# Both transposes of an expert unit put side by side, and the first two projection tiles run in lockstep

## The chip, the cores and the metric

The kernel runs on one core of a Trainium2 chip (trn2). The metric is the device time of one launch in microseconds.

## The reference

One step of a hybrid decoder layer for 1,024 prompt tokens and 8 sample tokens, width 1,024, all in float32. Conditioning rows come from a small product (`silu(c) @ w_ada + b_ada`, 9 rows, 6 vectors of 1,024 each: shift, scale and gate for each of two sub-layers). Two parts of it matter here.

```python
def modulate(x, shift, scale):
    return layer_norm(x) * (1.0 + scale) + shift

proj = u @ w_in                      # u: 1032 x 1024, w_in: 1024 x 4624
...
def expert_block(args):              # rows of one block, weights of one of 32 experts
    xb, e = args
    hb = jax.nn.silu(xb @ w_gate[e]) * (xb @ w_up[e])
    return hb @ w_down[e]
```

After normalising and modulating, the tokens are projected; an RG-LRU, a state space part and an output projection follow. Then each token goes to two of 32 experts (gate and up 1,024 x 512, down 512 x 1,024), and the two results are added with their weights.

## The kernel before, in words

**The start.** The tokens are normalised and transposed to `uT` (8 slices of 128 features). The conditioning for shift and scale is computed in four pairs: `ada_pair(c)` on TensorE (L889) multiplies, VectorE adds the bias row `badaP` to give `modP` (L1176), TensorE transposes it (L902), VectorE copies it to `ssT` (L1178) and modulates slices 2c and 2c+1 (L1184). All this is `u_pair(c)` (L1174). The projection runs in a split form: each float32 operand is split in a high and a low part, and three products are made (`PARTS`). ScalarE makes the high parts (L721 of a slice, L713 `w_high` of a tile's weights) and VectorE the low ones (`u_low` L1190, `w_low` L1152). A projection tile is 128 columns of `w_in`: 8 slices of 9 matmuls (L939). Tile 0 is made slice by slice as slices come (`by_slice`), with pairs 2 and 3 of the conditioning between its slices; then tiles 1 to 7 follow, each with two pieces of late conditioning behind it (`ada`, L877: gates and the second sub-layer's rows, added to the bias `bada4` in `mod_out`, L1244), then tiles 8 to 11. Tile t uses PSUM banks and weight buffers of parity t % 2. `lam_rates` (L1121) computes small vectors that the RG-LRU needs later. SyncE issues the weight loads in the order of L410 to L433: the tile's weights for t + 2 wait for the low part of tile t, and the two late loads behind them wait for the late pair before. POOL issues the bias rows (L512 to L519) and small rows first of all.

**The expert loop.** Rows of tokens are grouped in units of 32 rows of one expert; an expert has one or more units, 82 in all here. For each unit POOL gathers the rows (L1851, a quarter of a row on each partition, started by `icur`, which VectorE copies in `gather_rows`, L2589), TensorE transposes them (`x_turn`, L2207), VectorE copies them to `xT` (`x_out`, L2577), TensorE makes gate and up in four column tiles of 32 (`gate_up`, L2219), ScalarE copies them to `hb` (L1990), TensorE transposes that (`h_turn`, L2228), ScalarE takes a tanh (L1995), VectorE makes the product in two instructions (`h_out`, L2581, L2585), TensorE multiplies with the down weights (`down`, L2237), ScalarE copies the result (L2000) and POOL scatters it (L1859). The working copy of the weights `wcur` is filled from a ring where a unit begins a new expert: ScalarE copies gate weights (L2020) and VectorE up weights (L2619, `up_copy`), each chunk when the unit before has used its old one, and VectorE the down weights (L2632, `down_copy`) when `down` of the unit before is done. VectorE also reads the plan of the next unit into registers (`up_look`). SyncE loads three gate and up slots and two down slots of the ring, waiting for these copies. The order on each engine is written out by hand; TensorE's is

```python
                        h_turn(j * 2 + b)
                        gate_up(j * 2 + (b + 1))
                        x_turn(j * 2 + (b + 2), j + 1, b)
                        down(j * 2 + b)
```

and VectorE's is `h_out`, `up_copy` (with `x_out` of the unit after next between its second and third chunk), `gather_rows`, `scatter_rows`, `down_copy`, `up_look`.

## Time and profile before

| what | value |
|---|---|
| median of 3 runs | 1520.05 us (1520.03 to 1522.19) |
| the profiled execution | 1519.19 us, its span 1517.4 us |
| TensorE busy | 1361.2 us, 90% of the span |
| VectorE busy | 969.7 us, 64% |
| ScalarE busy | 574.1 us, 38% |
| POOL busy | 296.7 us, 20% |
| HBM traffic | 244 GB/s over the span |
| granted TensorE clock, mean | 0.951 |
| matmuls of gate and up (L2219) | 306.4 us busy |
| matmuls of down (L2237) | 158.6 us busy |
| up copies (L2619) | 124, 692 ns each |
| copies of down weights (L2632) | 31, 2409 ns each |
| gathers (L1851) | 84, 1226 ns each on POOL |

The profile is of one execution; its own time is 0.9 us below the median of the runs. Times in the rows further down are us from the start of the span, unless ns is written. A row of the timeline gives start, duration, engine, line, operation, what it writes and reads, and in brackets how long the engine had been idle and what ended that. PE is TensorE's matmuls, PEld its weight loads, DVE is VectorE, ACT ScalarE, SPq a DMA issue by SyncE. The granted clock is a share of TensorE's full 2.4 GHz; the lower of its two levels, 1.2 GHz, is 0.50.

### The profile page before, as it was taken

The numbers are of one execution on the slowest core, as the hardware profiler recorded it, in microseconds if no ns is written. First come the engines' busy times: TensorE is split into PE (matmuls) and PEld (weight loads), VectorE is DVE, ScalarE is ACT, GpSimd is POOL, SyncE is SP. The second block draws the span as 40 slices with busy tenths as digits, with TensorE's granted clock in tenths as the row PEclk, the third lists the DMA queues.
The fourth block names the chain that finished last, engine by engine and source line by source line (L and its number), as shares of the span: only waits on it lengthen the run. The fifth ranks groups of instructions, "written<-read, shape, count | busy, mean of one in ns | idle before, by whom it ended". The sixth has DMA issues, their size and how long they took to land.

```text
span 1517.4 us, 38240 instructions
## 1 busy us (share of the span) xinstructions
PE 1361.2 (90%) x13487; PEld 1007.3 (66%) x13487; DVE 969.7 (64%) x1720; ACT 574.1 (38%) x886; POOL 296.7 (20%) x325
## 2 busy tenths in 40 slices
PE   4799999999999999799999539999999899999964
PEld 3688989899888889578588525554455455555421
DVE  6755553958999998888687674544454353351649
ACT  4322232535655555732132104433343243241532
POOL 4000002211000000200000013443333343443310
PEclk9899999999999999899999759999999999999987
DMA  9666414644333434932332948999999988979683
GB/s 279 220 228 247 144 42 157 210 154 143 114 113 114 123 117 155 337 105 70 99 90 81 367 187 321 416 409 415 413 409 398 404 356 367 400 283 416 265 322 153
DMA packets 145042, 365.87 MB, mean 241 GB/s; under 512 B 16072, under 2 KB 94976, under 8 KB 117192
## 3 DMA queue, kind: packets, MB, share of 16 engines
q1 hardware_dynamic: 126072, 308.72, 54.6%
q0 software_dynamic: 18320, 54.08, 10.0%
q10 hardware_dynamic: 576, 2.10, 0.4%
q8 instruction: 45, 0.74, 0.2%
q14 instruction: 29, 0.24, 0.0%
HBM read 324.06 MB, written 45.63 MB: 244 GB/s over the span
## 4 chain that ended last, share of the span: by engine, by line
PE 31%; DMA 16%; DVE 7%; issue 2%; SPq 1%; ACT 1%; ACTq 0%; DVEq 0%; POOLq 0%
DMA ring<-in_w_up_dram 14%; PE PS L2088 10%; PE PS L2219 10%; PE PS L2237 5%; DMA ring<-in_w_down_dram 2%; PE PS L2228 1%; DVE big L2289 1%; PE PS L2119 1%; PE PS L2207 1%; PE PS L2154 1%; DVE ring L2687 1%; DVE ring L2692 1%; PE PS L2111 1%; DVE ring L2701 1%; DVE big_end L2301 1%
## 5 line engine op out<-in xcount | busy, mean ns | idle before, releaser
L939 PE MATMUL PS<-big 128*128 128x344 f32 x2592 | 425.2, 324 | 1.7 <-DVE big L1192 1.7
L939 PEld LDWEIGHTS PS<-big 128*128 128x128 f32 x2592 | 414.2, 190 | 10.5 <-issue 6.7
L2219 PE MATMUL PS<-ring,arena 128*32 128x256 f32 x5248 | 306.4, 386 | 0.5 <-DVE arena L2577 0.5
L2219 PEld LDWEIGHTS PS<-ring,arena 128*32 128x32 f32 x5248 | 164.3, 111 | 113.5 <-issue 6.5
L2020 ACT ACTIVATE ring<-ring 128x1024 f32 x124 | 124.0, 1049 | 94.1 <-PE PS L2219 52.4
L2237 PE MATMUL PS<-ring,arena 128*32 128x256 f32 x2624 | 158.6, 382 | 1.0 <-DVE arena L2585 1.0
L1851 POOL DMA_INDIRECT arena<-v_d,icur x84 | 103.0, 1226 | 283.1 <-DVE icur L2589 191.3
L1859 POOL DMA_INDIRECT f_d<-arena,scur x82 | 107.7, 1313 | 55.3 <-issue 48.6
L2237 PEld LDWEIGHTS PS<-ring,arena 128*32 128x32 f32 x2624 | 77.0, 109 | 57.1 <-issue 13.4
L2581 DVE SCALAR_TENSOR_TENSOR arena<-arena,PS 128x128 f32<-128x128 f32 x82 | 23.6, 288 | 135.4 <-ACT arena L1995 97.5
L2577 DVE COPY arena<-PS 128x256 f32<-128x256 f32 x82 | 34.7, 423 | 103.9 <-PE PS L2207 103.8
L2619 DVE COPY ring<-ring 128x1024 f32 x124 | 80.6, 692 | 25.7 <-SPq L1712 20.0
L1990 ACT ACTIVATE arena<-PS 128x256 f32<-128x256 f32 x82 | 31.4, 382 | 170.2 <-PE PS L2219 170.2
L2088 PE MATMUL PS<-low 128*128 128x512 f32 x256 | 83.7, 409 | 10.5 <-issue 4.9
L2632 DVE COPY ring<-ring 128x4096 f32 x31 | 74.7, 2409 | 28.6 <-PE PS L2237 28.6
L2088 PE MATMUL PS<-big,low 128*128 128x512 f32 x256 | 81.3, 400 | 0.0
L2088 PE MATMUL PS<-low,big 128*128 128x512 f32 x256 | 81.0, 398 | 0.0
L2000 ACT ACTIVATE arena<-PS 128x256 f32<-128x256 f32 x82 | 31.4, 383 | 100.5 <-PE PS L2237 96.4
L2088 PEld LDWEIGHTS PS<-low 128*128 128x128 f32 x256 | 47.4, 194 | 21.7 <-issue 8.1
L1154 DVE TENSOR_TENSOR big<-arena,big 128x1024 fp32r<-128x1024 f32 x20 | 24.5, 1224 | 56.6 <-ACT big L713 56.5
L2228 PEld LDWEIGHTS PS<-ident,arena 128*128 128x128 f32 x164 | 26.0, 207 | 50.7 <-issue 29.6
L2228 PE MATMUL PS<-ident,arena 128*128 128x128 f32 x164 | 41.9, 338 | 16.9 <-ACT arena L1990 16.7
(473 smaller groups left out, 1876.5 us busy)
## 6 DMA issues: line engine op xcount, KB each, us to landing
ring<-in_w_gate_dram SPq DMA_DIRECT2D x32, 2048.0 KB, 9.6
ring<-in_w_up_dram SPq DMA_DIRECT2D x32, 2048.0 KB, 14.9
ring<-in_w_down_dram SPq DMA_DIRECT2D x32, 2048.0 KB, 8.1
arena<-in_w_ada_dram SPq DMA_DIRECT2D x16, 1024.0 KB, 6.7
arena<-in_w_in_dram SPq DMA_DIRECT2D x20, 512.0 KB, 7.8
upper<-in_w_ada_dram SPq DMA_DIRECT2D x8, 1024.0 KB, 11.6
upper<-in_w_in_dram SPq DMA_DIRECT2D x16, 512.0 KB, 4.0
arena<-acs_d SPq DMA_DIRECT2D x8, 1024.0 KB, 4.9
```

The source lines that it names most:

```text
L939: mm = pe.matmul(PS[:, 3 * b + a, 0:CU], wss[b][:, i, k, :], us[:, j, k, a * CU:(a + 1) * CU], start=(k == 0 and (i, j) == PARTS[0]), stop ...
L1851: gp.indirect_dma_start(xg[b], None, v_q, bass.IndirectOffsetOnAxis(ap=icur[b][:, :], axis=0), bounds_check=QW * (SEQ + DEC) - 1, oob_is_e ...
L1859: gp.indirect_dma_start(f_q, bass.IndirectOffsetOnAxis(ap=scur[b][:, :], axis=0), yo[b], None, bounds_check=QW * 2 * (SEQ + DEC) - 1, oob_ ...
L1990: act.activation(hb, PS[:, 3, 0:FH], ACT.Copy).then_inc(hb_ready, 1)
L2020: act.activation(wcur[:, 1024 * q:1024 * q + 1024], ring[:, bass.ds(w + 1024 * q, 1024)], ACT.Copy).then_inc(gate_copied, 1)
L2088: mm = pe.matmul(PS[:, bank + n, :], (yh[h % 2], yl3[h % 3])[a][:, k, :], (WH, WL)[b][i][:, 512 * n:512 * n + 512], start=(k == 0 and (a, ...
L2219: mm = pe.matmul(PS[32 * g:32 * g + 32, 3, 0:FH], xT[:, c, CAP * q:CAP * q + CAP], wcur[:, w:w + FH], start=(q == 0 and c == 0), stop=(q = ...
L2228: mm = pe.transpose(PS[:, 4, P * c:P * c + P], hb[:, c::2], ident[:, :])
L2237: mm = pe.matmul(PS[32 * g:32 * g + 32, 6, 0:DQ], hT[:, c % 2, CAP * (c // 2):CAP * (c // 2) + CAP], wcur[:, 8192 + 1024 * c + DQ * g:8192 ...
L2577: ve.tensor_copy(xT, PS[:, 0, 0:2 * P].rearrange("p (c t) -> p c t", c=2)).then_inc(xT_ready, 1)
L2619: ve.tensor_copy(wcur[:, 4096 + 1024 * q:5120 + 1024 * q], ring[:, bass.ds(w + (4096 + 1024 * q), 1024)]).then_inc(up_copied, 1)
L2632: ve.tensor_copy(wcur[:, GU:GU + DN], ring[:, bass.ds(w, DN)]).then_inc(down_copied, 1)
```

## The change

In the expert loop `x_turn` of the unit after next stands directly behind `h_turn`, ahead of `gate_up`. The turned rows have two buffers, `xT[0]` and `xT[1]`. On VectorE `x_out` and `gather_rows` come first in a unit, ahead of `h_out`, and out of `up_copy`. The first three and last two units are ordered in the same way.

At the start tiles 0 and 1 are projected together, slice by slice: slice k of tile 0, then slice k of tile 1. The transposition of a conditioning pair (`ss_turn`) is taken out of `ada_pair` and stands behind the next even slice of tile 0; it writes to another part of the pair's own PSUM bank. The weights of tile 1 are loaded ahead of pair 1, and split on ScalarE behind the first slice and on VectorE behind pair 1. `lam_rates` moves behind all slices. The late conditioning starts behind both tiles, so that each of its pairs comes one tile later. The bias rows are loaded later: `badaP` after two token tiles are transposed, into their space, and `bada4` after the last pair has landed.

```diff
@@ -206,7 +206,7 @@
-        modP, badaP = at(46300, 4, P), at(43904, 4, P)
+        modP, badaP = at(46300, 4, P), at(15790, 4, P)
@@ -409,9 +410,9 @@
                 load_pair(0)
                 load_w(COL_XBC, 0)
+                load_w(COL_XBC + P, 1)
                 load_pair(1)
                 load_pair(2)
-                load_w(COL_XBC + P, 1)
                 load_pair(3)
@@ -509,14 +510,6 @@
-                for g in range(4):
-                    gp.dma_start(bada4[32 * g:32 * g + 32, :, :],
...
-                for g in range(4):
-                    gp.dma_start(badaP[32 * g:32 * g + 32, :, :],
...
@@ -551,9 +544,19 @@
                 gp.tensor_copy(qidx[:, :], itmp[:, :]).then_inc(gpsimd_once, 1)
+                gp.wait_ge(xnT_mm, 2)
+                for g in range(4):
+                    gp.dma_start(badaP[32 * g:32 * g + 32, :, :],
...
                 gp.wait_ge(xnT_mm, NT)
                 for b in range(2):
                     gp.memset(xb2[b][:, 0:3], 0.0).then_inc(gpsimd_once, 1)
+                gp.wait_ge(pair_loaded[3], 32)
+                for g in range(4):
+                    gp.dma_start(bada4[32 * g:32 * g + 32, :, :],
...
@@ -714,7 +717,7 @@
                 w_high(0, 0)
                 for k in range(KT):
-                    if k == 5:
+                    if k == 1:
                         w_high(1, 0)
@@ -890,16 +893,17 @@
                     if c > 1:
                         pe.wait_ge(mod0_ready, c - 1)
+                        pe.wait_ge(ss_ready, c - 1)
...
                     mm.then_inc(ada_mm, 1)
+
+                def ss_turn(c):
                     pe.wait_ge(mod0_ready, c + 1)
-                    if c > 1:
-                        pe.wait_ge(ss_ready, c - 1)
-                    pe.transpose(PS[:, 4 + c % 2, 0:P], modP[:, c, :], ident[:, :]).then_inc(ss_mm, 1)
+                    pe.transpose(PS[:, 6 + c % 2, P:2 * P], modP[:, c, :], ident[:, :]).then_inc(ss_mm, 1)
@@ -919,41 +923,57 @@
                 ada_pair(0)
+                ss_turn(0)
                 ada_pair(1)
...
-                for t in range(KT):
-                    if t > 1:
-                        pe.wait_ge(px_copied[t % 2], t // 2)
-                    project_split(t % 2, t // 2, by_slice=(t == 0))
-                    if t == 0:
-                        pe.wait_ge(mod0_ready, 4)
+                for k in range(KT):
+                    c = k // 2
+                    if k in (2, 4):
+                        ada_pair(c + 1)
+                    pe.wait_ge(uh_ready, k + 1)
+                    pe.wait_ge(ul_ready, k + 1)
+                    for b in range(2):
+                        if k == 0:
+                            pe.wait_ge(wh_ready[b], 1)
+                            pe.wait_ge(wl_ready[b], 1)
+                        mm = slice_products(b, k)
+                        if k == KT - 1:
+                            mm.then_inc(proj_mm[b], 1)
+                        if b == 0 and k % 2 == 0 and c < 3:
+                            ss_turn(c + 1)
+                pe.wait_ge(mod0_ready, 4)
+                pe.wait_ge(ss_ready, 4)
+
+                def late_pair(t):
                     for n in (2 * t, 2 * t + 1):
                         pe.wait_ge(late_loaded[n % 2], 16 * (n // 2) + 16)
                         ada(6 + n // KT, n % KT, late[n % 2]).then_inc(late_mm, 1)
-                with pe.Fori(4, 6) as i:
-                    for b in range(2):
-                        pe.wait_ge(px_copied[b], i)
-                        project_split(b, i)
+
+                late_pair(0)
+                for t in range(2, 12):
+                    pe.wait_ge(px_copied[t % 2], t // 2)
+                    project_split(t % 2, t // 2)
+                    if t < 9:
+                        late_pair(t - 1)
@@ -1194,16 +1213,15 @@
                 u_pair(0)
                 w_low(0, 0)
                 u_low(0)
+                u_pair(1)
+                w_low(1, 0)
                 u_low(1)
-                u_pair(1)
                 u_low(2)
                 u_low(3)
-                lam_rates()
                 u_pair(2)
                 u_low(4)
                 u_low(5)
                 u_pair(3)
-                w_low(1, 0)
                 u_low(6)
                 u_low(7)
@@ -1242,6 +1261,9 @@
                 def mod_out(r):
+                    if r == 1:
+                        ve.wait_ge(bada4_loaded, 64)
+                        step(ve.tensor_scalar(bada4[0:64, 2, :], bada4[0:64, 2, :], 1.0, None, ALU.add))
@@ -1495,7 +1517,7 @@
-        xT = at2(6784, 2, P)
+        xT = [at2(6784, 2, P), at2(8064, 2, P)]
@@ -2201,13 +2223,13 @@
                 def x_turn(u, j, b):
+                    pe.wait_ge(xT_ready, u)
                     pe.wait_ge(xg_loaded[b], j * 16 + 16)
-                    pe.wait_ge(xT_ready, u)
@@ -2242,21 +2264,21 @@
                 with pe.Fori(1, pairs) as j:
                     for b in range(2):
                         h_turn(j * 2 + b)
-                        gate_up(j * 2 + (b + 1))
                         x_turn(j * 2 + (b + 2), j + 1, b)
+                        gate_up(j * 2 + (b + 1), 1 - b)
                         down(j * 2 + b)
@@ -2571,10 +2593,13 @@
-                def x_out(u):
+                def x_out(u, b):
                     ve.wait_ge(eT_mm, u + 1)
-                    ve.wait_ge(gu_mm, u * QW)
-                    ve.tensor_copy(xT, PS[:, 0, 0:2 * P].rearrange("p (c t) -> p c t", c=2)).then_inc(xT_ready, 1)
+                    ve.tensor_copy(xT[b], PS[:, 0, 0:2 * P].rearrange("p (c t) -> p c t", c=2)).then_inc(xT_ready, 1)
+
+                def x_out_next(u, b):
+                    ve.wait_ge(gu_mm, (u - 1) * QW)
+                    x_out(u, b)
@@ -2613,14 +2638,11 @@
                         for q in range(QW):
-                            if q == 2:
-                                x_out(u)
                             ve.wait_ge(gu_mm, before * QW + (q + 1))
...
@@ -2657,9 +2681,10 @@
                 with ve.Fori(1, pairs) as j:
                     for b in range(2):
+                        x_out_next(j * 2 + (b + 2), b)
+                        gather_rows(j * 2 + (b + 4), b)
                         h_out(j * 2 + b)
                         up_copy(j * 2 + (b + 2), j * 2 + (b + 1))
-                        gather_rows(j * 2 + (b + 4), b)
                         scatter_rows(j * 2 + b, j, b)
                         down_copy(j * 2 + (b + 1))
                         up_look(j * 2 + (b + 3))
```

## Rows read from the trace of the kernel before

**Rows 1.** Windows: span; busy us (instructions) of PE, PEld, DVE, ACT, POOL; clock; DMA; GB/s.

```profile
1050.00:1100.00 50.00, 46.35 (x724) 24.98 (x720) 23.00 (x52) 17.83 (x33) 18.51 (x15) 0.97 1.01 412
...
1406.00:1414.00 8.00, 8.00 (x130) 4.47 (x133) 3.62 (x9) 5.83 (x10) 2.55 (x3) 1.00 0.16 38
```

**Rows 2.** Chain of waits: start us, us, what (expert loop, the longest pieces).

```profile
1185.62 5.17 PE PS L2219 x64
...
1421.19 10.16 DMA ring<-in_w_down_dram
```

**Rows 3.** Chain of waits, one unit of the expert loop.

```profile
1272.54 1.86 PE PS L2237 x32
1274.40 0.44 PE PS L2228 x2
1274.84 3.59 PE PS L2219 x64
1278.43 0.37 PE PS L2207 x2
```

**Rows 4.** Timeline, TensorE: start us, us, engine, line, operation, tiles (the last units).

```profile
1441.93 0.51 PE L2228 MATMUL PS<-ident,arena 128*128 128x128 f32 x2
...
1447.68 0.50 PE L2228 MATMUL PS<-ident,arena 128*128 128x128 f32 x2
```

**Rows 5.** Timeline, weight loads of eight full transposes at the start.

```profile
30.13 0.86 PEld L885 LDWEIGHTS PS<-ident,arena 128*128 128x128 f32 x8 [1.45 <-DVE arena L1141]
```

**Rows 6.** Groups of instructions by line, 1185 to 1424 us: busy us, mean ns.

```profile
L2632 DVE COPY ring<-ring 128x4096 f32 x12 | 28.3, 2358 | 6.7 <-PE PS L2237 6.7
...
L2228 PE MATMUL PS<-ident,arena 128*128 128x128 f32 x76 | 19.4, 338 | 6.4 <-ACT arena L1990 6.4
```

**Rows 7.** Timeline, a unit with a copy of down weights.

```profile
1286.85 0.51 PE L2228 MATMUL PS<-ident,arena 128*128 128x128 f32 x2
...
1287.75 2.63 POOL L1851 DMA_INDIRECT arena<-v_d,icur  x1 [1.41 <-ACT arena L2000]
...
1290.12 0.29 DVE L2581 SCALAR_TENSOR_TENSOR arena<-arena,PS 128x128 f32<-128x128 f32 x1 [0.63 <-issue]
```

**Rows 8.** Timeline, a plain unit: copy of turned rows, then the gather.

```profile
1272.68 0.42 DVE L2577 COPY arena<-PS 128x256 f32<-128x256 f32 x1 [2.42 <-PE PS L2207]
...
1274.17 1.02 POOL L1851 DMA_INDIRECT arena<-v_d,icur  x1 [3.56 <-DVE icur L2589]
```

**Rows 9.** Timeline, the gather for which TensorE waited.

```profile
914.14 1.00 POOL L1851 DMA_INDIRECT arena<-v_d,icur  x1 [2.63 <-DVE icur L2589]
...
921.48 0.20 PEld L2207 LDWEIGHTS PS<-ident,arena 128*128 128x128 f32 x2 [0.41 <-DMA arena<-v_d,icur]
```

**Rows 10.** Timeline, VectorE at the third token tile.

```profile
16.10 1.29 DVE L1132 BATCH_NORM_STATS2 lnst<-arena 128x6 f32<-128x512 f32 x2 [0.94 <-DMA arena<-in_x_prompt_dram]
```

**Rows 11.** Timeline, TensorE from the first slices to the late conditioning behind tile 1.

```profile
47.84 4.61 PE L939 MATMUL PS<-big 128*128 128x344 f32 x18
...
52.38 1.96 PE L895 MATMUL PS<-upper 128*32 128x128 f32 x64
...
72.42 11.63 PE L939 MATMUL PS<-big 128*128 128x344 f32 x72
...
83.98 1.92 PE L877 MATMUL PS<-arena,upper 128*32 128x512 f32 x16
```

**Rows 12.** Waits, 47.8 to 84 us: us in total, times, longest.

```profile
PE PS L902 <- DVE upper L1176: 5.5, 3, 2.2
```

**Rows 13.** Windows, while the first slices are projected.

```profile
48.80:52.00 3.20, 3.20 (x13) 3.20 (x12) 2.70 (x6) 2.02 (x2) 0.00 (x0) 0.50 1.09 369
```

**Rows 14.** Timeline and groups by line, VectorE: low parts and modulation.

```profile
45.00 2.37 DVE L1192 TENSOR_TENSOR big<-arena,big 128x1032 fp32r<-128x1032 f32 x2
...
L1184 DVE TENSOR_SCALAR arena<-arena,ssT 128x1024 f32<-128x1024 f32 x8 | 6.5, 812 | 0.1
```

**Rows 15.** Page, DMA issues: KB each, median us from issue to landing.

```profile
arena<-in_w_in_dram SPq DMA_DIRECT2D x20, 512.0 KB, 7.8
```

More of the change, by code:

```diff
@@ L921, in _, with slice_products, project_split @@
                 ada_pair(0)
+                ss_turn(0)
                 ada_pair(1)
                 PARTS = ((0, 0), (0, 1), (1, 0))
-                def project_split(b, w_round, by_slice=False, half_way=None):
+                def slice_products(b, k):
+                    for i, j in PARTS:
+                        for a in range(3):
+                            mm = pe.matmul(PS[:, 3 * b + a, 0:CU], wss[b][:, i, k, :], us[:, j, k, a * CU:(a + 1) * CU],
+                                           start=(k == 0 and (i, j) == PARTS[0]),
+                                           stop=(k == KT - 1 and (i, j) == PARTS[-1]))
+                    return mm
+                def project_split(b, w_round, half_way=None):
                     pe.wait_ge(wh_ready[b], w_round + 1)
@@ L931, in project_split @@
                             half_way()
[L932 to L949 removed]
+                        mm = slice_products(b, k)
+                    mm.then_inc(proj_mm[b], 1)
+                for k in range(KT):
[8 more added lines that the diff above has]
+                            pe.wait_ge(wl_ready[b], 1)
+                        mm = slice_products(b, k)
+                        if k == KT - 1:
[5 more added lines that the diff above has]
+                def late_pair(t):
                     for n in (2 * t, 2 * t + 1):
@@ L1230, in conv_tile @@
                         .then_inc(xo_ready[b], 1)
+                lam_rates()
                 ve.wait_ge(uh_ready, KT + 1)
@@ L2244, in _ @@
                 x_turn(0, 0, 0)
[L2245 removed]
+                gate_up(0, 0)
                 x_turn(1, 0, 1)
@@ L2622, in up_copy @@
                         ve.sem_inc(up_copied, QW)
-                        x_out(u)
                 def down_copy(u):
@@ L2639, in _ @@
                 ve.sem_inc(down_copied, 1)
-                x_out(0)
+                x_out(0, 0)
                 gather_rows(2, 0)
@@ L2645, in _ @@
                 up_copy(1, 0)
+                x_out(1, 1)
                 gather_rows(3, 1)
```

36 lines of the change are left out of this document (13 added, 23 removed).

## The prediction

> **What bounds the kernel now.** I read the chain of waits first, then the timeline of the stretches that it names, then windows for DMA and clock, and last the lists of one engine. The diff touches two places: the start (to about 86 us) and the expert loop (about 913 to 1452 us).
>
> In the expert loop DMA and TensorE take turns as the bound. Until 1184.9 us the chain runs through the loads of expert weights, and DMA is saturated there (share 1.01, 412 GB/s); later there are holes (share 0.16 at 1406 us) [rows 1]. From 1185.6 us the chain is TensorE alone, to the last load of a down matrix at 1421 us [rows 2]. A unit there is four pieces: down 1.86, turn of the hidden rows (L2228) 0.44, gate and up 3.59, turn of the token rows (L2207) 0.37, together 6.26 us [rows 3]. 38 units lie in 1185 to 1424 us, 12 of them with a copy of down weights (L2632, 2.36 us each) [rows 6].
>
> At the start TensorE waits for VectorE: three waits of 5.5 us in sum for the conditioning rows, while tile 0 is projected slice by slice [rows 12]; tile 1 follows with nothing to wait for.
>
> **Part 1, one stretch of turns.** What does a switch between 32-column tiles and the whole array cost? The second last unit has no token turn: from its hidden turn to the next is 1447.68 - 1441.93 = 5.75 us, against 6.26 [rows 3, 4]. So a token turn with its two switches costs 0.51. The change keeps the two transposes, beside two others of their form: eight weight loads of a full transpose take 0.86 us, 0.107 each [rows 5], so 0.21 for two. A unit becomes 5.96 us, 0.30 less. Bounds: 0.14 (two transposes priced at the whole 0.37) and 0.37 (they vanish); I take 0.28, near the measured 0.51 - 0.21, with 0.02 for what a mixed stretch may still cost.
>
> What is queued behind? The copy of turned rows (x_out, L2577, 0.42 us) now stands on VectorE ahead of h_out, on which `down` waits. In a plain unit it can run once the two turns are done, some 0.9 us after the hidden turn began (an estimate from 0.44 + 0.21 and a wait), and h_out ends near 2 us, against the 4.1 us worked out below at which TensorE wants it: free. In a unit with a down copy VectorE is held: h_out starts 1290.12 - 1286.85 = 3.27 us after the hidden turn [rows 7]. Now x_out and the index copy (together about 0.45) go first, h_out's two instructions take 0.6, and hT is there at about 4.35 plus 0.05. Gate and up with no turn behind it took 5.75 - 0.44 - 1.86 = 3.45, so TensorE is ready at 0.44 + 0.21 + 3.45 = 4.1. So it waits 0.3 and nothing is gained there; bounds: nothing lost, and 0.8 where two such units follow each other and up copies (4 at 0.7) pile up. I take a loss of 0.05 against before.
>
> The gather is the other moved wait: x_turn(u+2) now wants its rows before gate and up, 3.6 us sooner; but the index copy that starts the gather moves forward as much, no longer behind the up copies. x_out to POOL's instruction takes 1274.17 - 1272.68 = 1.5 us [rows 8]; the one gather for which TensorE waited began at 914.14 and was turned at 921.48, so 7.2 us [rows 9]. The loop x_turn, x_out, gather, x_turn is 0.5 + 1.5 + 7.2 = 9.2 us, and it has two units, 11.9. Slack 2.7, hidden. That first gather is late by 3 us now, since TensorE reaches it after the turn of 0.44 instead of after 3.6 more; the DMA-bound stretch covers this, as it does all units before 1184.9: the saturated loads set when the 41st unit (82 in all, less 38 and 3 last ones) has its weights, and a faster TensorE waits longer. If that cover were thinner, up to 0.28 x 41 = 11 us more would be gained; I take 0.
>
> Sum: 26 plain units x 0.28 - 12 x 0.05 = 6.7 us, plus 0.3 for the last: **7.0 us**. DMA has holes for it. Bounds 2.5 (plain units at 0.14, 12 losing 0.1) and 11.7 (39 x 0.30).
>
> The Trainium skill (TensorEngine Tiling (Array Packing), Key Properties) says that changing the tiling mode drains TensorE. By that rule alone one switch pair less a unit is saved everywhere, which gives the upper bound, 11.7; the trace has a second term that it leaves out, the hidden rows that `down` waits for.
>
> **Part 2, the two tiles in lockstep.** Durations: a slice of one tile is 9 matmuls, 72 in 11.6 us, so 1.44 each [rows 11]; a conditioning pair 1.96; a turn of it about 0.3. VectorE: a low part 1.19, a modulation 0.81, a pair of them with the small ones about 2.3 [rows 14].
> Before, tile 1 ended at 84.0, with late conditioning of 1.9 (L877) between the tiles [rows 11]; without it, 82.1. Now slice 0 of tile 0 starts when its low part is there, 45.00 + 1.19 = 46.2; it ends at 47.7, and the turn, now behind it, at 48.0. VectorE then does pair 1 (50.3) and the low weights of tile 1, moved forward (1.2; 51.5). TensorE idles 3.5 us. From 51.5 remain 15 slices (21.6), two pairs (3.9), two turns (0.6): 77.6. VectorE's own list stays ahead: lam_rates (3.3 us) went behind it. After an idle stretch the granted clock was 0.50, the lower of two levels, for 3.2 us, and 18 matmuls took 4.61 instead of 2.9 [rows 11, 13]; one such spell costs 1.7: 79.3. So the gain is 82.1 - 79.3 = 2.8; with 0.3 for switches, **2.5 us**. Bounds: 4.4 (no slow spell) and -0.5 (two spells and 1.5 of late low parts).
> Late conditioning moves one tile later, and SP with it: the weights of tile t+2 are now requested after the late pair behind tile t. They land 7.8 us after issue [rows 15], that is 1.9 + 0.5 + 7.8 = 10.2 us after tile t; ScalarE's split and copy and VectorE's low part (about 1 to 1.2 us each, two of them one behind the other) make it 12.8. TensorE wants them at 1.9 + 11.6 + 1.9 = 15.4. Slack 2.6: free, and gone if a load takes 10.4.
> The bias rows: 1 MB of broadcasts leaves the first 7 us of POOL's queue. VectorE waited 0.94 us for the third token tile at 16.10 [rows 10], and is paced by itself afterwards. That wait ends, and the first tile may come sooner: **1.2 us** (0 to 2.5). badaP is now issued near 20 us and needed near 39; bada4 is issued when the last pair has landed and needed at the first mod_out, past 120 us, where its +1 costs VectorE about 0.4 us beside TensorE's next tile. Both I cost at nothing; if badaP were late, the whole chain would be, us for us.
>
> **Total**: 7.0 + 2.5 + 1.2 = 10.7 us. The profiled execution took 1519.19 us (span 1517.4), 0.9 below the median of 1520.05; from the median, **1509.3**.
>
> **Rivals.**
> (a) The loop gains nothing: h_out behind x_out makes `down` wait in more than the 12 units, or loads fill DMA's holes first. For it: 3.27 us above. Against: plain units have 2 us of room. Time 1520.05 - 3.7 = 1516.4.
> (b) The start gains nothing: TensorE's idle 3.5 us just moves, and two slow spells follow. For it: the chain pair, turn, modulation, low part is as long as before and now carries a weight split. Time 1520.05 - 7.0 = 1513.
> (c) Slower: the gather takes the place of the switch. VectorE's copies and POOL's gather exclude each other: one beside L2632 took 2.63 us [rows 7]. The index copy now comes just before four up copies, so POOL's work may wait 2.6 us. In a unit with a down copy x_out is held 2.8 us, so the loop is 2.8 + 1.5 + 7.2 + 0.1 = 11.6, and with 2.6 more 14.2, against 11.9: 2.3 us, in 12 units 28, less 10.7: 1537. It decides from a wait of 1.2 us in each of those 12 units (14.4 us, past what both parts bring plus 3); the plain units have 2.7 of slack. The Trainium skill (SBUF — State Buffer, the "DVE blocks DMA" trap) says that a copy in a fast mode locks GpSimd out, so that it can't write descriptors. By that rule the wait is as long as the copy that runs, 0.7 for an up copy, since the lock is free between them; the trace's 2.63 agrees for the long one.
> (d) Neither part does anything: 1520.
>
> **Chances.** Both parts work, 0.62; (a) 0.14; (b) 0.10; (c) 0.09; (d) 0.05. About 0.2% (3.0 us) is what a measurement of this kernel can tell from no change. (a) is faster by 3.7, narrowly: I count 0.10 of it as faster and 0.04 as the same. So faster 0.62 + 0.10 + 0.10 = 0.82, same 0.04 + 0.05 = 0.09, slower 0.09. The range takes the upper ends of both parts short of all at once (1502) and reaches (a) and part of (d): 1519.
>
> **What would show it.** Hidden turns 5.95 to 6.0 us apart in plain units, 6.2 to 6.3 with a down copy, where TensorE waits for L2585; one stretch of four transposes; the chain of TensorE alone beginning near 1185 us less only what the start brings. At the start: one idle stretch of 3 to 4 us before tile 1's first slice, then none; the loads of tile weights never in TensorE's waits. Wrong would be: TensorE waiting for v_d rows (c), that beginning earlier by more than 3 us beyond it, or tile 2 not 3 us earlier.

## The result, and the profile after

The changed kernel takes **1526.95 us** (median of 21, 1522.38 to 1533.69) against 1521.41 (1519.65 to 1524.51, 21) for the kernel before on the same chip: ratio 1.0038, 95% interval 1.0028 to 1.0049. It is slower by 5.5 us, where 10.7 us less were forecast. Its profiled execution took 1529.8 us (span 1528.2), 2.9 above its median, and that of before 1519.19 (span 1517.4), so the two traces differ by 10.8 us where the medians differ by 5.5. Part of what the traces show is the spread of single executions.

The page of the kernel after: its span, busy times, and the shares of the chain.

```profile
span 1528.2 us, 38110 instructions
...
PE 1366.3 (89%) x13487; PEld 1035.4 (68%) x13487; DVE 969.3 (63%) x1720; ACT 573.7 (38%) x886; POOL 280.2 (18%) x325
...
PE 32%; DMA 14%; DVE 7%; issue 4%; SPq 1%; DVEq 1%; ACT 0%; ACTq 0%; POOLq 0%
```

**The start** went as forecast, and better. Timeline of TensorE's weight loads (start us, us, engine, line, operation, tiles, and in brackets the idle time before and its releaser; L934 is the projection, L899 a conditioning pair, L880 late conditioning):

```profile
49.49 5.73 PEld L934 LDWEIGHTS PS<-big 128*128 128x128 f32 x27 [3.63 <-issue]
55.44 1.69 PEld L899 LDWEIGHTS PS<-upper 128*32 128x32 f32 x64 [0.21 <-issue]
...
66.75 9.88 PEld L934 LDWEIGHTS PS<-big 128*128 128x128 f32 x63
76.84 0.16 PEld L880 LDWEIGHTS PS<-arena,upper 128*32 128x32 f32 x8 [0.22 <-issue]
...
78.70 11.35 PEld L934 LDWEIGHTS PS<-big 128*128 128x128 f32 x72 [0.84 <-issue]
```

One idle stretch of 3.6 us (forecast 3.5), one slow spell behind it (27 loads in 5.73 us where 27 later ones take 4.3), then none. Tiles 0 and 1 end at 76.8, forecast 79.3; before, without the late conditioning between the tiles, it was 82.1.

**The loop** did not. One pair of rows tells it: the turns of the hidden rows (hidden turns, for short) of the 41st and the 79th unit, 38 units apart, in the kernel before and then after (timeline, weight loads):

```profile
1184.92 0.32 PEld L2228 LDWEIGHTS PS<-ident,arena 128*128 128x128 f32 x2 [6.89 <-ACT arena L1990]
...
1424.57 0.32 PEld L2228 LDWEIGHTS PS<-ident,arena 128*128 128x128 f32 x2 [0.41 <-ACT arena L1990]
```

```profile
1184.85 0.32 PEld L2250 LDWEIGHTS PS<-ident,arena 128*128 128x128 f32 x2 [1.29 <-ACT arena L2012]
...
1434.39 0.32 PEld L2250 LDWEIGHTS PS<-ident,arena 128*128 128x128 f32 x2 [0.41 <-ACT arena L2012]
```

239.65 us became 249.54, where about 233 were forecast. A plain unit (one with no copy of down weights) was 6.26 us [rows 3]; here is one after the change, with the turns (L2250, L2229) now together, gate and up (L2241), down (L2259) and the next unit's turn:

```profile
1388.40 0.31 PEld L2250 LDWEIGHTS PS<-ident,arena 128*128 128x128 f32 x2 [0.41 <-issue]
1388.63 0.26 PEld L2229 LDWEIGHTS PS<-ident,arena 128*128 128x128 f32 x2
1389.05 2.75 PEld L2241 LDWEIGHTS PS<-ring,arena 128*32 128x32 f32 x56 [0.17 <-issue]
1392.12 0.17 PEld L2241 LDWEIGHTS PS<-ring,arena 128*32 128x32 f32 x4 [0.32 <-issue]
1392.85 0.17 PEld L2241 LDWEIGHTS PS<-ring,arena 128*32 128x32 f32 x4 [0.57 <-issue]
1392.95 1.80 PEld L2259 LDWEIGHTS PS<-ring,arena 128*32 128x32 f32 x32
1395.16 0.31 PEld L2250 LDWEIGHTS PS<-ident,arena 128*128 128x128 f32 x2 [0.41 <-issue]
```

The unit lasts 6.76 us, not 5.96. The turns are as forecast, but behind 56 of the 64 loads TensorE stops for 0.32 and then 0.57 us with nothing that the profile names as its releaser ("issue"). Nor is it a wait for the copies of new weights: this unit has none. 24 of these 38 units have such a pause (counted as under the table further down). What else happens then? GpSimd, same unit, scatter (L1881) and gather (L1873):

```profile
1390.08 1.04 POOL L1881 DMA_INDIRECT f_d<-arena,scur  x1 [4.42 <-DVE icur L2614]
1391.42 1.02 POOL L1873 DMA_INDIRECT arena<-v_d,icur  x1 [0.31 <-issue]
```

The gather is issued 0.3 us behind the scatter's end, and TensorE stops 0.4 us after that. Read over all units of this trace, nearly all with a gather that close behind a scatter have a pause, mostly of 0.6 to 0.9 us in all, from about 0.4 to 1.4 us behind the gather's issue, in gate and up or in down, whichever runs; units where 0.6 us or more lie between the two have none, also where the gather is issued inside gate and up (six of them). In the kernel before, the gather of a plain unit was issued at its end ([rows 8]) and the scatter early in the next unit.

**The first unit.** The chain of waits at the loop's opening, kernel after (parts):

```profile
909.43 0.43 DVE arena L2598
...
910.77 6.98 DMA arena<-v_d,icur
...
917.88 0.66 PE PS L2229 x2
918.54 5.91 PE PS L2241 x64
```

As forecast, TensorE waits for the first gather; it came to 12.0 us for that unit instead of 6.3, part of it gate and up at the lower clock (granted 0.50 from 918.5 to 921.5 us; 5.91 us instead of 3.59).

### The profile page after: what moved, and what is told of

The parts are those of the page before. It is cut to its first block, busy times and chain, and to the rows that moved or that the text cites. A ratio compares the mean times of both kernels' runs of the same rounds, so it can differ in the third digit from the quotient of the medians.

```text
span 1528.2 us, 38110 instructions
## 1 busy us (share of the span) xinstructions
PE 1366.3 (89%) x13487; PEld 1035.4 (68%) x13487; DVE 969.3 (63%) x1720; ACT 573.7 (38%) x886; POOL 280.2 (18%) x325
## 4 chain that ended last, share of the span: by engine, by line
PE 32%; DMA 14%; DVE 7%; issue 4%; SPq 1%; DVEq 1%; ACT 0%; ACTq 0%; POOLq 0%
DMA ring<-in_w_up_dram 10%; PE PS L2110 10%; PE PS L2241 10%; PE PS L2259 5%; DMA ring<-in_w_down_dram 2%; PE PS L2250 1%; DVE big L2311 1%; PE PS L2141 1%; PE PS L2176 1%; DVE ring L2712 1%; PE PS L2229 1%; DVE ring L2717 1%; PE PS L2133 1%; DVE ring L2726 1%; DVE big_end L2323 1%
## 5 line engine op out<-in xcount | busy, mean ns | idle before, releaser
L934 PE MATMUL PS<-big 128*128 128x344 f32 x2592 | 424.6, 324 | 6.0 <-DVE big L1174 3.4
L934 PEld LDWEIGHTS PS<-big 128*128 128x128 f32 x2592 | 413.2, 190 | 15.4 <-issue 9.9
L2241 PE MATMUL PS<-ring,arena 128*32 128x256 f32 x5248 | 323.0, 385 | 4.5 <-issue 1.8
L2241 PEld LDWEIGHTS PS<-ring,arena 128*32 128x32 f32 x5248 | 167.9, 111 | 133.9 <-issue 39.2
L2259 PE MATMUL PS<-ring,arena 128*32 128x256 f32 x2624 | 174.5, 380 | 5.8 <-DVE arena L2610 2.6
L1881 POOL DMA_INDIRECT f_d<-arena,scur x82 | 100.8, 1229 | 307.2 <-ACT arena L2022 241.1
L2259 PEld LDWEIGHTS PS<-ring,arena 128*32 128x32 f32 x2624 | 106.3, 109 | 56.3 <-DVE arena L2610 15.2
L2654 DVE COPY ring<-ring 128x4096 f32 x31 | 71.0, 2291 | 61.7 <-PE PS L2259 59.5
L1873 POOL DMA_INDIRECT arena<-v_d,icur x84 | 93.1, 1109 | 60.6 <-DVE icur L2614 31.4
L2110 PEld LDWEIGHTS PS<-big,low 128*128 128x128 f32 x256 | 49.4, 193 | 11.0
L2110 PEld LDWEIGHTS PS<-low,big 128*128 128x128 f32 x256 | 49.2, 192 | 10.8
L2250 PEld LDWEIGHTS PS<-ident,arena 128*128 128x128 f32 x164 | 25.8, 206 | 44.1 <-issue 29.2
```

Source lines behind the costliest of these rows:

```text
L934: mm = pe.matmul(PS[:, 3 * b + a, 0:CU], wss[b][:, i, k, :], us[:, j, k, a * CU:(a + 1) * CU], start=(k == 0 and (i, j) == PARTS[0]), stop ...
L1873: gp.indirect_dma_start(xg[b], None, v_q, bass.IndirectOffsetOnAxis(ap=icur[b][:, :], axis=0), bounds_check=QW * (SEQ + DEC) - 1, oob_is_e ...
L1881: gp.indirect_dma_start(f_q, bass.IndirectOffsetOnAxis(ap=scur[b][:, :], axis=0), yo[b], None, bounds_check=QW * 2 * (SEQ + DEC) - 1, oob_ ...
L2110: mm = pe.matmul(PS[:, bank + n, :], (yh[h % 2], yl3[h % 3])[a][:, k, :], (WH, WL)[b][i][:, 512 * n:512 * n + 512], start=(k == 0 and (a, ...
L2241: mm = pe.matmul(PS[32 * g:32 * g + 32, 3, 0:FH], xT[b][:, c, CAP * q:CAP * q + CAP], wcur[:, w:w + FH], start=(q == 0 and c == 0), stop=( ...
L2250: mm = pe.transpose(PS[:, 4, P * c:P * c + P], hb[:, c::2], ident[:, :])
```

## The experiments

Each kernel is compared with the kernel before on one chip, and the comparisons were made on five chips (called P to T), none of them known to be that of the result. Ratios are to the kernel before, with the 95% interval; they need not be those of the two medians (start_only: 0.9971, medians 1513.07 and 1516.53 us, 0.9977). "38 units" is the stretch of the rows above, "pauses" are those counted in the whole loop: places inside gate and up or down where two weight loads start 0.5 us or more apart (another way of counting changes a number by one or two). The kernel before was profiled once, and its chip isn't on record.

```
kernel             chip  ratio (interval)          38 units  pauses
changed, result     -    1.0038 (1.0028, 1.0049)   249.5     41
gather_late         P    0.9948 (0.9927, 0.9969)   231.0      0
first_behind        P    0.9937 (0.9921, 0.9953)   230.3      0
start_only          P    0.9971 (0.9961, 0.9982)   240.6      0
loop_only           P    0.9983 (0.9971, 0.9996)   231.5      0
after_again         Q    1.0032 (1.0014, 1.0050)   248.7     40
h_out_first         Q    1.0027 (1.0006, 1.0049)   246.1     15
best1               Q    0.9953 (0.9934, 0.9973)   235.8      0
best2               Q    1.0004 (0.9988, 1.0020)   245.4     17
after_b             R    1.0031 (1.0016, 1.0046)   249.3     36
first_behind_b      R    1.0038 (1.0024, 1.0051)   249.3     39
loop_only_b         R    1.0085 (1.0067, 1.0103)   249.5     38
gather_late_b       R    0.9931 (0.9911, 0.9952)   235.4      0
swap_before         S    1.0014 (0.9998, 1.0029)   241.4      0
loop_late           S    0.9976 (0.9962, 0.9989)   231.3      0
start_only_b        S    0.9973 (0.9958, 0.9989)   239.6      0
first_and_late      S    0.9937 (0.9915, 0.9959)   231.0      0
after_c             T    1.0060 (1.0046, 1.0074)   249.4     38
swap_before_b       T    1.0099 (1.0086, 1.0112)   256.8     30
kernel before       -                              239.7      0
```

### Chip P: is it the gather, the first unit, or one part alone?

**gather_late** holds the gather (GpSimd, `u` counts four units ahead):

```
-                def gather(u, b):
+                def gather(u, b, late=False):
                     gp.wait_ge(icur_ready, u + 1)
+                    if late:
+                        gp.wait_ge(gu_mm, (u - 3) * QW + 4)
...
-                        gather(j * 2 + (b + 4), b)
+                        gather(j * 2 + (b + 4), b, True)
```

> The changed kernel; only the gathers of the loop (GpSimd) wait besides until the first four of eight gate and up slices of the unit running on TensorE are done, so the gather starts some 3.7 us into a unit and no longer within 0.3 us of the scatter's end. Theory A (a gather issued straight behind a scatter stops TensorE for 0.7 to 0.8 us, which is what makes plain units 6.76 us long): the pauses go, plain units last 5.96 us, some 25 of them behind 1185 us give back up to 15 us, less what the weight transfers then hold up: 1512 to 1518 us. Rival B (TensorE's own instruction stream pauses because the second turn no longer breaks it, whatever GpSimd does): plain units stay at 6.76 us, 1526 to 1528 us.

The edit holds it longer than this says: `gu_mm` counts four for a whole gate and up (`QW` is 4), so the gather waits for all of the running one, not for half of it.

**first_behind**: in the two units written out ahead of the loop, `gate_up(u + 1, 1 - u)` stands ahead of `x_turn(u + 2, 1, u)` again.

> The changed kernel; only in the two units written out ahead of the loop the token turn stands behind gate and up again. Theory C (the first unit of the changed kernel, 12.0 us against 6.3 us, waits for its gather, and those 5.8 us push every weight transfer of the stretch that the transfers bound): the first unit is 6 to 8 us again, the weights land 4 to 6 us earlier, and the kernel gains 3 to 5 us: 1522 to 1524 us. Rival D (the transfers of that stretch cover the late start, as the prediction had it): under 1 us, 1526 to 1527.5 us.

**start_only** and **loop_only** are the diff's two halves (its hunks ahead of the expert phase, and those in it).

> The part of the change ahead of the experts alone, with the expert loop of the kernel before. The changed kernel's projections of tiles 2 and 3 stand 7.1 us earlier by the trace, its loop 3.4 us earlier. Theory E (what the start gains carries through the bound of the weight transfers, whose stream begins earlier too): 1515 to 1518.5 us, 3 to 6 us under the kernel before. Rival F (the stretch that the transfers bound ends at the same time whatever comes before it): 1520.5 to 1522 us.

> The part of the change in the expert loop alone, with the start of the kernel before. If the two parts add up, this one costs what the changed kernel lost (5.5 us) and what the start part gained: with theory E for the start 1529 to 1532 us, with rival F 1526.5 to 1528 us. The forecast for this part, a gain of 7 us, would be 1514 us.

gather_late: 1508.1 us against 1516.53, below theory A's band in microseconds because this chip's kernel before is 5 us faster too. But loop_only and first_behind had no pauses either, and both have the new order with gathers as close (start_only, with the old loop, says nothing on this). Here is a plain unit of loop_only, weight loads and then GpSimd, with a gather as close behind the scatter as in the result:

```profile
1200.94 0.32 PEld L2228 LDWEIGHTS PS<-ident,arena 128*128 128x128 f32 x2 [0.41 <-issue]
1201.16 0.26 PEld L2207 LDWEIGHTS PS<-ident,arena 128*128 128x128 f32 x2
1201.59 3.18 PEld L2219 LDWEIGHTS PS<-ring,arena 128*32 128x32 f32 x64 [0.17 <-issue]
1204.86 1.64 PEld L2237 LDWEIGHTS PS<-ring,arena 128*32 128x32 f32 x32
1206.91 0.31 PEld L2228 LDWEIGHTS PS<-ident,arena 128*128 128x128 f32 x2 [0.41 <-issue]
```

```profile
1202.66 1.03 POOL L1859 DMA_INDIRECT f_d<-arena,scur  x1 [2.28 <-ACT arena L2000]
1203.99 1.03 POOL L1851 DMA_INDIRECT arena<-v_d,icur  x1 [0.30 <-issue]
```

The unit lasts 5.97 us, the forecast's number to a hundredth, and the 38 units 231.5. So these four runs decide nothing on theory A: the pauses may belong to the changed program as a whole, or to the chip. first_behind is at first sight what theory C expects, but its band was for a kernel with pauses, and the changed kernel did not run on P. For the start theory F fell (ratio 0.9971, 4.4 us of 1516.5; 3.5 between the medians); loop_only gained 2.6 us by its ratio (1.9 between the medians): it is neither of its two theories, which had it slower than before, nor the forecast's 7 us.

### Chip Q: the changed kernel again, and candidates

> The changed kernel itself, word for word, once more. Neither part alone, nor the whole with another order in the first two units, showed a pause in the loop: all their plain units last 5.97 us. Theory G (the pauses of 0.7 to 0.8 us belong to this very program, in which TensorE's loop and GpSimd's meet in one way): they are there again, plain units 6.7 us, and the kernel is slower than before by about 5 us. Rival H (they belong to the chip or the execution of that first profile and not to the program): plain units 5.97 us, no pauses, and the parts add up: 5 us under the kernel before, ratio 0.996 to 0.997.

**h_out_first** exchanges on VectorE (in the loop and the two units ahead of it):

```
-                        x_out_next(j * 2 + (b + 2), b)
-                        gather_rows(j * 2 + (b + 4), b)
                         h_out(j * 2 + b)
+                        x_out_next(j * 2 + (b + 2), b)
+                        gather_rows(j * 2 + (b + 4), b)
```

> The changed kernel with one exchange on VectorE: the gated rows (h_out) before the copy of the turned tokens (x_out) and the gather index in every unit. Theory I (in some 20 units behind a weight copy, down products wait 0.2 to 0.5 us for h_out, because x_out and the index copy, 0.57 us together, stand before it): those waits fall to under 0.1 us and the kernel gains 4 to 6 us on the changed one, less what the transfers hold up. Rival (the token copy or the gather is then late): slower by 1 us or more.

**best1** is gather_late, first_behind and h_out_first together, **best2** the same without gather_late.

> Three edits on the changed kernel together: token turn behind gate and up in the first two units, h_out first on VectorE, and the loop's gathers held until four of eight slices are done. If the gains over the changed kernel add up (first units 3 to 4 us, h_out 3 us): ratio to the kernel before 0.989 to 0.992. If the held gather only costs: 0.992 to 0.995.

> As the one before, without holding the gathers. If a gather right behind a scatter costs nothing (no pauses were seen with it in three of four kernels), it is the same as that one within 1 us: ratio to the kernel before 0.989 to 0.992; if pauses come back, plain units 6.7 us and a ratio above 1.

The pauses are back in the changed kernel (40), which goes against rival H as far as it blamed one execution, but not as far as it blamed the chip. (The "three of four kernels" in best2's expectation are two: only loop_only and first_behind had run a gather right behind a scatter without pauses.)

h_out_first brought nothing that its interval can tell, though the waits that theory I names did go: down products waited 6.5 us for h_out in the 38 units of after_again and 0.9 here. Its own rival took part of that back. A gather issued beside the copy of down weights of the 57th unit lands 8.8 us after its issue, TensorE stands before the token turn of the 58th, and the two units take 17.0 us where after_again takes 14.0. The same happens in best1 (chain of waits; L2231 is the token turn):

```profile
1283.31 8.45 DMA arena<-v_d,icur
...
1291.89 0.66 PE PS L2231 x2
```

The gathers of h_out_first and best2 lie at more than one distance from the scatter, so these two traces show where the pauses end. Where no copy of down weights runs beside the two, 28 of 37 gathers at 0.42 to 0.52 us have idle weight loads of 0.2 us or more behind them, many shorter than the count takes, and none of 35 at more than 0.52 us.

best2 came out as its second case, with pauses and a ratio of 1.0004. best1, with held gathers, is faster than the kernel before by 0.47%, where both its bands lay lower (the nearer one at 0.992 to 0.995, just beside it); the gains do not add up, and the 58th unit, 10.4 us long in best1, is a part of why. best2 and h_out_first differ by the first two units alone: 1.0004 against 1.0027 on the same chip, 17 and 15 pauses, a first unit of 6.9 us against 11.1. That is some 3.5 us for theory C, though the two intervals overlap.

### Chip R: all on one chip

> The changed kernel word for word, now beside the same kernels that showed no pause, all four on one chip. Theory J (whether TensorE pauses is a matter of the chip: on some a gather issued 0.3 us behind a scatter stops it, on others not): this kernel and the two next to it behave alike, either all with pauses (plain units 6.7 us, ratios 1.002 to 1.006) or all without (5.97 us, this one at 0.994 to 0.997). Theory G (it is a matter of this program): this one alone has pauses, with some 40 of them and a ratio of 1.002 to 1.006.

> The same with the token turn behind gate and up in the first two units; without pauses in its first run (ratio 0.9937). Theory J: pauses exactly if the changed kernel beside it has them. Theory G: none again, ratio 0.992 to 0.996.

> The loop part alone; without pauses in its first run (ratio 0.9983). Theory J: pauses exactly if the changed kernel beside it has them, then with a ratio of 1.005 to 1.009. Theory G: none again, ratio 0.997 to 1.000.

> The changed kernel with the loop's gathers held until four of eight slices are done; no pause in its first run (ratio 0.9948). Theory A (the pause comes from a gather straight behind a scatter): none on this chip either, also if the three beside it have them, ratio 0.993 to 0.997. Rival: if they pause and this one does too, the gather is not the cause.

Theory J holds: two kernels that had no pause on P have 39 and 38 here, word for word the same programs, and go from 0.9937 to 1.0038 and from 0.9983 to 1.0085. loop_only_b, one plain unit and its GpSimd rows:

```profile
1201.29 2.75 PEld L2219 LDWEIGHTS PS<-ring,arena 128*32 128x32 f32 x56 [0.17 <-issue]
1204.35 0.16 PEld L2219 LDWEIGHTS PS<-ring,arena 128*32 128x32 f32 x3 [0.32 <-issue]
1205.14 0.19 PEld L2219 LDWEIGHTS PS<-ring,arena 128*32 128x32 f32 x5 [0.63 <-issue]
```

```profile
1202.35 1.02 POOL L1859 DMA_INDIRECT f_d<-arena,scur  x1 [2.31 <-ACT arena L2000]
1203.67 1.02 POOL L1851 DMA_INDIRECT arena<-v_d,icur  x1 [0.30 <-issue]
```

The changed kernel and first_behind_b are equal here (1.0031, 1.0038). That is a weak test of theory C: the first unit of after_b took 8.8 us and not 12.0, against 8.1 in first_behind_b.

And theory A holds beside it: gather_late_b, on the same chip, has no pause, and differs from the changed kernel by the held gather alone (0.9931 against 1.0031, 15 us; 14.3 between the medians). Its rows, weight loads and then GpSimd (L1883 scatter, L1875 gather):

```profile
1394.17 0.32 PEld L2252 LDWEIGHTS PS<-ident,arena 128*128 128x128 f32 x2 [0.41 <-issue]
1394.39 0.26 PEld L2231 LDWEIGHTS PS<-ident,arena 128*128 128x128 f32 x2
1394.82 3.18 PEld L2243 LDWEIGHTS PS<-ring,arena 128*32 128x32 f32 x64 [0.17 <-issue]
```

```profile
1390.21 1.03 POOL L1883 DMA_INDIRECT f_d<-arena,scur  x1 [1.76 <-DVE icur L2616]
1393.40 1.02 POOL L1875 DMA_INDIRECT arena<-v_d,icur  x1 [2.16 <-PE PS L2243]
1396.13 1.02 POOL L1883 DMA_INDIRECT f_d<-arena,scur  x1 [1.71 <-ACT arena L2024]
```

Between the scatter's end (1391.24) and the gather lie 2.2 us. The gather comes 5.2 us into its unit, behind the whole of gate and up, not 3.7 as I had written, and behind the first unit no token turn waits for it even so.

### Chips S and T: does it take the new order on TensorE?

**swap_before** is the kernel before with this alone (GpSimd):

```
-                        gather(j * 2 + (b + 4), b)
                         scatter(j * 2 + b, b)
+                        gather(j * 2 + (b + 4), b)
```

> The kernel before; only GpSimd's loop issues the scatter of a unit ahead of the gather of the unit four further on, where the gather stood first, so the gather now follows at once on the scatter's end, inside gate and up. The order on TensorE and VectorE stays. Theory A (adjacent scatter and gather stop TensorE, whatever its own order): on a chip that pauses, pauses of 0.7 to 0.8 us in most units, 7.0 us instead of 6.26 us a unit, 15 us or more: ratio 1.008 to 1.015; on a chip that doesn't, 0.999 to 1.003. Theory K (it takes the new, denser order on TensorE too): no pause on either, 0.999 to 1.003.

> The loop part alone with its gathers held. If the pauses are all that was wrong with the forecast of the loop part (7 us), this is 1 to 7 us under the kernel before on any chip (the first unit of 8 to 12 us takes 3 to 5 us back): ratio 0.995 to 0.999. If other waits take the gain: 1.000 or above.

> The start part alone, on another chip than its first run (ratio 0.9971, 3.5 us under the kernel before, where 3.7 us was forecast). There is no new order in its loop, so it should not care for the chip: ratio 0.996 to 0.998. If its ratio is 1.000 or above, the start part depends on the chip too.

> The changed kernel with its gathers held and the token turn behind gate and up in the first two units. If the late first unit costs something besides the pauses, this beats the kernel with the held gathers alone (0.9948, 0.9931) by 2 to 4 us: ratio 0.990 to 0.992. If the transfers cover it, 0.993 to 0.995.

On S swap_before had no pause, and with no kernel beside it that pauses, that decided nothing. So it ran again beside the changed kernel:

> The changed kernel word for word, as the control for the run beside it. On a chip that pauses: some 40 pauses, plain units 6.7 us, ratio 1.002 to 1.006. On one that doesn't: none, 0.994 to 0.997.

> The kernel before with the scatter ahead of the gather on GpSimd, again. Read only beside the control. If the control pauses and theory A holds: pauses here too, units of about 7 us, ratio 1.008 to 1.015. If the control pauses and theory K holds (it takes the denser order on TensorE too): no pause, 6.26 us, 1.000 to 1.003. If the control doesn't pause, this stays open.

On T the control pauses (1.0060), and so does the kernel before with its gather behind its scatter: 1.0099, 15 us slower, by one exchange of two lines on GpSimd. Weight loads and GpSimd of one plain unit of it, which lasts 7.10 us instead of 6.26:

```profile
1379.32 0.31 PEld L2228 LDWEIGHTS PS<-ident,arena 128*128 128x128 f32 x2 [0.41 <-issue]
1379.76 2.75 PEld L2219 LDWEIGHTS PS<-ring,arena 128*32 128x32 f32 x56
1382.89 0.14 PEld L2219 LDWEIGHTS PS<-ring,arena 128*32 128x32 f32 x3 [0.38 <-issue]
1383.60 0.18 PEld L2219 LDWEIGHTS PS<-ring,arena 128*32 128x32 f32 x5 [0.57 <-issue]
```

```profile
1380.81 1.01 POOL L1859 DMA_INDIRECT f_d<-arena,scur  x1 [3.52 <-ACT arena L2000]
1382.12 1.04 POOL L1851 DMA_INDIRECT arena<-v_d,icur  x1 [0.30 <-issue]
```

That is theory A without the new order: K falls. (Some of its units also wait for the gather, which this exchange delays: the one ratio on S, 1.0014, says that this is a small part.)

But "pauses in most units" was too much: all but two of its gathers follow a scatter within 0.31 us, and there are only 30 pauses. The trace says where they are missing. Beside 29 of these pairs VectorE copies down weights, the scatter takes 1.3 to 2.1 us instead of 1.0, and not one has a pause; of the 48 others 32 are followed by idle weight loads of 0.2 us or more, inside gate and up or down. A scatter and a gather close together are needed for the pause, then, but are not enough.

loop_late and start_only_b came as expected (0.9976 and 0.9973; the start part gave the same on both chips it ran on, P and S, neither of which pauses). first_and_late came at 0.9937, inside the band for "the transfers cover it" and among the kernels with held gathers alone. Those ran on other chips, and their first unit took 9.2 and 9.3 us, only some 1 us more than the 8.1 here, so this too says little on theory C.

**The version to use** is the changed kernel with held gathers: 0.9948 and 0.9931, and, with the first token turns behind gate and up, 0.9937, on three chips; of these R is one where the changed kernel itself is slower than before.

## Why the prediction was wrong

Forecast 1509.3 us (1502 to 1519), measured 1526.95, on the other side of the kernel before.

**The step that failed** is the one on the gather: "the index copy that starts the gather moves forward as much ... Slack 2.7, hidden." It asked only whether the rows still come in time. They do: behind the first unit the list of waits names no gather. It did not ask what the gather, now 3.0 us into the unit and no longer 6.0, would stand beside on GpSimd, and so put that at nothing. It had stood alone at the end of the unit; it now follows the scatter at once, because the scatter of the unit before is the instruction that held GpSimd at that moment. On a chip where this stops TensorE that costs 0.8 us in a plain unit (6.76 us, not 5.97). In the 38 units: 231.5 us (loop_only on P) plus 24 pauses of about 0.75 are about 249.5, and 249.54 were measured. Over the whole kernel, to hold the gather gave 15 us back on R; the result missed the forecast by 17.6. With the gathers held the changed kernel is 7.9 and 10.5 us under the kernel before by its ratios (P and R), where 10.7 was forecast.

**Without the pauses, point by point:**

- *A plain unit, 5.96 to 5.98 us*: 5.97 in loop_only, first_behind, gather_late. Right. The Trainium skill (TensorEngine Tiling (Array Packing), Key Properties) has it that a change of tiling mode drains TensorE; the trace agrees, with 0.29 us a unit gained by one pair of changes less.
- *Units with a down copy lose 0.05, waiting 0.3 for h_out*: right in size. The list of waits, weight loads, loop_only, 1193 to 1410 us (us in total, times, longest):

```profile
PEld PS L2237 <- DVE arena L2588: 3.8, 9, 0.6
```

  0.42 each. Putting h_out first (h_out_first) took these waits away and brought one of the gather instead (above).
- *38 units, 6.7 us less*: 8.1 less in loop_only (239.65 to 231.52), 8.7 in gather_late, 9.4 in first_behind; but 4.2 in gather_late_b, where down products waited 8.7 us for h_out, not 3.8. Right where TensorE has no pause.
- *"The DMA-bound stretch covers" the late first gather*: **wrong**, by some 3 us. The forecast had the first gather 3 us late; the first unit of loop_only takes 11.7 us instead of 6.3, and with it the first copy of down weights is late, which frees the slot of the next load. SyncE's DMA issues, kernel before and then loop_only:

```profile
919.46 0.38 SPq L1685 DMA_DIRECT2D ring<-in_w_gate_dram  x1
...
926.56 19.11 SPq L1691 DMA_DIRECT2D ring<-in_w_down_dram  x2
947.77 0.37 SPq L1685 DMA_DIRECT2D ring<-in_w_gate_dram  x1
```

```profile
918.02 0.38 SPq L1685 DMA_DIRECT2D ring<-in_w_gate_dram  x1
...
930.55 18.28 SPq L1691 DMA_DIRECT2D ring<-in_w_down_dram  x2
950.32 0.37 SPq L1685 DMA_DIRECT2D ring<-in_w_gate_dram  x1
```

  loop_only is 1.4 us ahead at the one gate load and 4.0 behind at the next down load: a saturated stretch covers what comes late only if it does not itself wait for what comes late. From the first hidden turn to the 41st the kernel before takes 267.4 us (917.5 to 1184.9), loop_only 270.9 (916.0 to 1186.9). With 8.1 gained behind it, some 4.7 should remain; measured are 2.6 (ratio 0.9983, up to 4.4 by its interval) and 3.6 (loop_late, 0.9976). Single traces spread, but all of them together say the same. This stretch takes 263.9 to 267.5 us in the five traces with the old order (mean 265.5), 266.6 to 270.9 in the ten with the new one (269.0), and 266.1 to 268.7 in the five where the first token turns are put back (267.1). So to put them back wins some 2 of these 3.5 us. In times only best2 against h_out_first shows it (3.5 us by the ratios); in the other pairs the two first units differ by about 1 us, not by 4. Theory C is likely, then, and not settled.
- *The start, 2.5 + 1.2 us*: 0.9971 and 0.9973 are 4.4 and 4.1 us of 1517 (3.5 and 4.1 between the medians). Right, at the upper side: one slow spell, as taken, and the low parts in time. The trace of after has tile 2 at 78.70, which is 7.1 us earlier than the kernel before; 1.9 of it is only the late conditioning that now comes behind; of the other 5.2 the earlier first pair (35.6 instead of 36.8) is 1.2.
- *The start's gain carries*: start_only_b reaches its first hidden turn at 911.6, the kernel before at 917.5; but over all traces it is 914.4 on the mean of fourteen with the new start (910.0 to 917.6) and 917.0 on that of six with the old one (915.4 to 918.7), so some 2.7 us. The changed kernel itself got there at 914.1, 917.6, 913.6 and 917.6 in its four profiles, so what seems lost between 92 and 905 us in the result's trace is within the spread between executions, some of it the clock (granted 1.00 and 0.98 below). Windows (span, busy us of the engines, granted clock, DMA, GB/s) of two profiles of the same changed kernel, the result's first:

```profile
300.00:500.00 200.00, 192.02 (x1341) 178.10 (x1341) 168.49 (x325) 106.81 (x113) 14.99 (x19) 1.00 0.41 127
```

```profile
300.00:500.00 200.00, 190.78 (x1314) 177.64 (x1314) 166.15 (x320) 105.13 (x118) 16.07 (x23) 0.98 0.40 123
```

**The rivals.** (a), (b) and (d) did not come about. (c) named the right instruction, the gather moved forward, and the right side, but another mechanism: it had TensorE wait for late rows because GpSimd is held by VectorE's copies. The rows came in time; and the Trainium skill's rule (SBUF — State Buffer, the "DVE blocks DMA" trap), which speaks of VectorE's copies in a fast mode, is not what acts here: beside the long copy that it fits (a gather of 2.63 us [rows 7]) there is no pause, and 29 of the 38 longest idle stretches in the result's trace (0.5 us or more) have no copy of weights beside them or within 1.5 us before. Nor did any rival have a stop of TensorE without a wait. That a rival lay on the measured side is luck: its mechanism did not act.

## What to carry to other kernels

When an instruction is moved, look not only at whether its result is still in time but at what it now follows on its own queue: here a gather 0.3 us behind a scatter stopped TensorE, on some chips. Keep them apart, by a wait on something that is already counted: at 0.6 us and more no pause was seen, at 0.5 still some. And a gain below 1% is to be measured on several chips: here the same program (first_behind) was 0.6% faster than the kernel before on one and 0.4% slower on another, and a control of known behaviour has to run beside each experiment.

## What the runs showed of the hardware

- On chips Q, R and T, and on that of the result, TensorE stops, for 0.7 to 0.8 us in a plain unit, when a gather is issued on GpSimd within about 0.3 us of the end of a scatter: behind 244 of 268 such gathers in the six traces with the new order there are 0.2 us or more of idle weight loads (0.28 to 0.42 us apart, no down copy beside them). On P it did not, in two kernels with that distance, and on S not in one. Beside a copy of down weights it did not on any chip. At 0.42 to 0.52 us 28 of 37 still had one, above that none of 35 (h_out_first, best2). What TensorE lacks meanwhile isn't known: the profile names no releaser, and which resource the two engines share was not tried. Nor was it tried whether the order (gather behind scatter) matters: in the trace of the kernel before 27 gathers are followed by a scatter with a distance as small, without a pause, but its chip isn't on record.
- Whether it is the chip as such, or something that differs between these machines, is open too; the programs were the same. The kernel before, whose one trace has no pauses, took 1516.5 and 1517.1 us on P and S against 1520.0 to 1522.4 us on the others. That these are the same two groups of chips is seen, not explained.
- A switch between 32-column tiles and the whole array shows as 0.41 us before the first load of a hidden turn ("0.41 <-issue" above) and 0.17 on the way back; to merge two such stretches saved 0.29 us a unit (6.26 to 5.97).
